# Prompt attention units dealt over the K pages and the V pages of a decoder layer, by one table of slots

## What is computed

```python
def layer_front(x, norm1_g, w_in, q_norm_g, k_norm_g):
    proj = rms_norm(x, norm1_g) @ w_in            # q, k, v, a, gate
    ...
    return q, k, v, a * jax.nn.sigmoid(gt)

# prompt: 8 heads, causal attention over the own and the past block of 256 keys (512 keys at most)
# sample: 2048 past keys in 16 pages of 128 keys per stream, best 3 blocks of 256 keys by q.mean(k),
#         plus the 4 new keys; pages are found by page_table
def conv_branch(u_ext, conv_w, conv_b, conv_norm_g):   # 31 taps, RMS norm over channels, swish
    ...
def layer_back(x, attn, conv, w_out, norm2_g, w_query, keys1, keys2, expert_u, expert_v):
    mix = jnp.concatenate([attn.reshape(x.shape[:-1] + (ATTN_WIDTH,)), conv], axis=-1)
    h = x + mix @ w_out
    return h + peer_ffn(rms_norm(h, norm2_g), w_query, keys1, keys2, expert_u, expert_v)
```

## Time and profile before

| what | value |
|---|---|
| time, median of 3 runs (lowest, highest) | 2172.93 us (2168.53, 2173.59) |
| the profiled execution's own time | 2174.22 us |
| its span, first to last instruction | 2172.6 us |
| mean granted TensorE clock | 0.964 |
| busy share of the span: TensorE matmul, weight load, VectorE, ScalarE, GpSimd | 93%, 88%, 63%, 34%, 35% |
| attention stage in the span | about 196 to 478 us |
| in it: K phase, to the last turn of a page | 196.0 to 372.5 us |
| in it: V phase, to the start of the last V chunk's product | 372.5 to 470.0 us |

### The profile page before, as it was taken

How to read it: one execution, slowest core, us unless ns; L and a number is a source line. 1 busy time by engine, 2 the same in 40 slices (tenths; PEclk the granted TensorE clock), 3 DMA queues, 4 the chain that set the end, 5 groups by cost and what they waited for, 6 DMA issues and landing times.

```text
span 2172.6 us, 39130 instructions
## 1 busy us (share of the span) xinstructions
PE 2025.2 (93%) x14822; PEld 1911.2 (88%) x14822; DVE 1371.3 (63%) x2452; ACT 729.7 (34%) x940; POOL 769.9 (35%) x493
## 2 busy tenths in 40 slices
PE   6878899768999999998899999999989999999999
PEld 6877667228999999998899999999989999999999
DVE  3869673301334457999888884200068988889885
ACT  3233565202222222322355554232222332333331
POOL 3222211323233333343321222333344555655550
PEclk9998999759999999999999999999999999999999
DMA  4252655971222333333244545533589999999993
GB/s 158 63 85 101 205 198 185 359 296 60 76 78 100 123 125 129 137 132 111 98 177 165 205 180 208 195 137 129 182 289 313 332 345 307 334 326 345 323 312 108
DMA packets 202168, 420.05 MB, mean 193 GB/s; under 512 B 28129, under 2 KB 137762, under 8 KB 189250
## 3 DMA queue, kind: packets, MB, share of 16 engines
q1 hardware_dynamic: 162866, 314.92, 42.1%
q0 software_dynamic: 32768, 100.75, 13.1%
q10 hardware_dynamic: 6416, 2.78, 1.0%
HBM read 350.46 MB, written 67.92 MB: 193 GB/s over the span
## 4 chain that ended last, share of the span: by engine, by line
PE 45%; issue 32%; DVE 9%; POOL 6%; DMA 3%; ACT 2%; DVEq 1%; SPq 1%; POOLq 1%; ACTq 0%
PE pair L1394 13%; PE pair L1396 12%; PE pair L1395 12%; POOL w_lo L552 6%; DVE conv L972 3%; PE pair L1539 2%; DVE pair L1355 1%; DVE w_lo L1338 1%; PE pair L1551 1%; DMA v_ring<-in_cache_v 1%; DMA picked_a<-acts,at_unit 1%; DMA page_ring<-in_cache_k 1%; PE pair L1504 1%; PE pair L1526 1%; DVEq L965 1%
## 5 line engine op out<-in xcount | busy, mean ns | idle before, releaser
L1394 PE MATMUL pair<-x_hi,w_hi 128*128 128x272 f32 x2560 | 757.4, 296 | 24.1 <-DVE x_lo L928 16.2
L1396 PE MATMUL pair<-x_hi,w_lo 128*128 128x272 f32 x2560 | 744.5, 291 | 0.0
L1395 PE MATMUL pair<-x_lo,w_hi 128*128 128x272 f32 x2560 | 741.0, 289 | 0.0
L552 POOL TENSOR_TENSOR w_lo<-w_raw,w_hi 128x2048 fp32r<-128x2048 f32 x64 | 301.3, 4707 | 621.7 <-ACT w_hi L798 621.7
L1394 PEld LDWEIGHTS pair<-x_hi,w_hi 128*128 128x128 f32 x2560 | 486.9, 190 | 27.7 <-issue 22.3
L1395 PEld LDWEIGHTS pair<-x_lo,w_hi 128*128 128x128 f32 x2560 | 487.1, 190 | 0.2
L1396 PEld LDWEIGHTS pair<-x_hi,w_lo 128*128 128x128 f32 x2560 | 485.7, 190 | 0.0
L1394 PE MATMUL pair<-a_hi,w_hi 128*128 128x416 f32 x1024 | 360.7, 352 | 13.1 <-DVE w_lo L1338 7.6
L1396 PE MATMUL pair<-a_hi,w_lo 128*128 128x416 f32 x1024 | 360.9, 352 | 0.0
L1395 PE MATMUL pair<-a_lo,w_hi 128*128 128x416 f32 x1024 | 358.2, 350 | 0.0
L816 ACT ACTIVATE act_out<-pair 128x544 f32<-128x544 f32 x128 | 81.3, 635 | 462.0 <-PE pair L1396 462.0
(11 more groups left out here) (199 smaller groups left out, 2644.4 us busy)
## 6 DMA issues: line engine op xcount, KB each, us to landing
w_raw<-in_u_t SPq DMA_DIRECT2D x64, 1024.0 KB, 5.8
acts<-act_out SPq DMA_DIRECT2D x64, 544.0 KB, 3.0
w_raw<-in_v_t SPq DMA_DIRECT2D x128, 256.0 KB
v_raw<-in_v_t SPq DMA_DIRECT2D x128, 256.0 KB, 5.9
gates<-g_out SPq DMA_DIRECT2D x13, 2048.0 KB, 8.0
g_in<-gates SPq DMA_DIRECT2D x16, 1664.0 KB, 13.3
act<-acts SPq DMA_DIRECT2D x64, 416.0 KB, 5.9
page_ring<-in_cache_k SPq DMA_DIRECT2D x64, 256.0 KB, 2.9
```

Source lines behind the costliest of these rows:

```text
L552: pool.tensor_tensor(w_lo[:, slot, :], w_raw[:, slot, :], w_hi[:, slot, :].bitcast(F32), ALU.subtract).then_inc(u_lo_done, 1)
L1394: te.matmul(out, s_hi, m_hi, start=start, stop=False)
L1395: te.matmul(out, s_hi, m_lo, start=False, stop=False)
L1396: return te.matmul(out, s_lo, m_hi, start=False, stop=stop)
```

## The change

A table `started` names the slot in which each prompt unit begins. 12 units begin in the K phase, at slots 2, 4, 7, 10, 12, 15, 18, 20, 23, 26, 28 and 31. The other 20 begin in the V phase, whose slots are counted from `FIRST_VALUES` (`at` = 0 to 31): at 0, 1, 2, 3, 5, 6, 7, 9, 10, 11, 13, 14, 15, 16, 18, 19, 20, 22, 23 and 24. All three engines now walk one loop over 65 slots, and one V chunk is attended in each slot of the V phase. The selection of batch 1, the convolution's norm and its swish stand at fixed slots of that loop. Since prompt units and V chunks now run together, the PSUM banks are dealt anew: probabilities are turned in banks 4 and 0, V products gather in bank 2, outputs are turned in bank 1, and the prompt keeps 3, 5, 6 and 7. `pages_pt` and `sqc` no longer lie over `q_t`, which the late units still read, but over the second halves of `w_hi` and `w_lo`. The number of matmuls, of activations and of VectorE operations on data stays the same; ScalarE's list has two more table loads.

```diff
@@ constants @@
+    S_TURN, O_TURN, O_OUT = (4, 0), 1, 2
...
+    FIRST_VALUES = CHUNKS + 1
+    LAST_SLOT = FIRST_VALUES + CHUNKS
...
+    KEY_UNITS, VALUE_SLOTS = 12, 26
+    started = {2 + CHUNKS * n // KEY_UNITS: n for n in range(KEY_UNITS)}
+    for n in range(UNITS - KEY_UNITS):
+        started[FIRST_VALUES + VALUE_SLOTS * n // (UNITS - KEY_UNITS)] = KEY_UNITS + n
@@ ScalarE @@
+            for t in range(LAST_SLOT):
+                if t < CHUNKS:
+                    keep_page(t, 0)
+                    keep_page(t, 1)
+                if t % 4 == 1 and 1 < t < CHUNKS:
+                    keep_scores(t // 4 - 1)
+                if t < CHUNKS:
+                    keep_page(t, 2)
+                    keep_page(t, 3)
+                if t in started:
+                    prompt_exp(started[t])
+                if t - 1 in started:
+                    prompt_keep(started[t - 1])
...
+                if t == CHUNKS:
+                    keep_scores(2 * PAGES // 4 - 1)
+                    keep_probabilities(0)
+                at = t - FIRST_VALUES
+                if at == 3:
+                    exp_rows(1)
+                if at in (4, 6, 8, 10):
+                    square_conv((at - 4) // 2)
+                if at == 13:
+                    root(pair[0], CH, sumc_done, CC, rootc_done)
+                if at == 15:
+                    sc.wait_ge(z_done, 1)
+                    for cc in range(CC):
+                        sc.activation(sig_c[:, cc, :], conv[:, cc, :], ACT.Sigmoid).then_inc(sigc_done, 1)
+                    keep_output(0)
+                    keep_probabilities(1)
@@ VectorE @@
+            for t in range(LAST_SLOT):
+                if started.get(t - 3, 0) % 2:
+                    prompt_mix(started[t - 3] // 2)
+                if t - 1 in started:
+                    prompt_norm(started[t - 1])
+                if t < CHUNKS:
+                    some_taps()
+                if t in started:
+                    prompt_max(started[t])
...
+                if at == 1:
+                    rows_mask(1)
+                if at == 2:
+                    rows_max(1)
+                if at == 5:
+                    rows_norm(1)
+                if at == 14:
+                    reciprocal_rms(rootc_done)
...
+                if 17 <= at < 17 + CC:
+                    finish_conv(at - 17)
@@ TensorE @@
             def turn_probabilities(b):
                 te.wait_ge(s_normed, b + 1)
+                if b:
+                    te.wait_ge(rootc_done, 1)
...
+            for t in range(LAST_SLOT):
+                if t < CHUNKS:
+                    turn_page(t, 0)
+                    turn_page(t, 1)
+                if t in started:
+                    prompt_scores(started[t])
+                if 1 <= t <= CHUNKS:
+                    score_chunk(t - 1)
+                if t - 1 in started:
+                    prompt_turn(started[t - 1])
+                if t < CHUNKS:
+                    turn_page(t, 2)
+                    turn_page(t, 3)
+                if t == CHUNKS:
+                    turn_probabilities(0)
+                at = t - FIRST_VALUES
+                if at >= 0:
+                    if at == PAGES:
+                        turn_probabilities(1)
+                    attend(at)
+                if t - 2 in started:
+                    prompt_values(started[t - 2])
+                if at in (5, 7, 9, 11):
+                    sum_block(pair[0], sqc, (at - 5) // 2, CC, sqc_done, sumc_done)
+                if at == PAGES + 2:
+                    turn_output(0)
```

More of the change, by code:

```diff
@@ L768, in _ @@
[L768 to L777 removed]
+                sc.activation(o_nat[:, :], bank(O_OUT), ACT.Copy).then_inc(o_kept, 1)
@@ L1120, in _, with finish_conv @@
                                 ALU.add).then_inc(own_kept, 1)
[L1121 to L1149 removed]
+            def finish_conv(cc):
                 v.wait_ge(sigc_done, cc + 1)
@@ L1153, in _ @@
                 parts(PAIRS + cc, conv[:, cc, :])
+            for t in range(LAST_SLOT):
[7 more added lines that the diff above has]
+                    prompt_max(started[t])
+                if t == PAGES + 2:
+                    rows_mask(0)
+                elif t == PAGES + 3:
+                    rows_max(0)
+                elif t == PAGES + 5:
+                    rows_norm(0)
+                at = t - FIRST_VALUES
+                if at == -1:
+                    assert next_tap == [TAPS, TAPS]
+                    v.drain()
+                    v.memset(stats[:, 56:57], 0.0).then_inc(conv_done, 1)
+                if at == 1:
[6 more added lines that the diff above has]
+                    reciprocal_rms(rootc_done)
+                    for cc in range(CC):
+                        last = v.scalar_tensor_tensor(conv[:, cc, :], conv[:, cc, :], conv_g[:, cc:cc + 1], rstd[:, :],
+                                                      ALU.mult, ALU.mult)
+                    last.then_inc(z_done, 1)
+                if 17 <= at < 17 + CC:
+                    finish_conv(at - 17)
             mix_output(0)
```

129 lines of the change are left out of this document (34 added, 95 removed).

## The result

The changed kernel takes **2184.84 us** (median of 5 runs, 2182.11 to 2188.78), the kernel before 2172.17 us (5 runs, 2168.53 to 2173.59). The ratio is 1.0061, 95% interval 1.0047 to 1.0075: slower by 12.7 us, where 6 us faster was forecast, and above the forecast's range. The profiled execution of the changed kernel has an own time of 2184.84 us and a span of 2183.2, the one of before 2174.22 and 2172.6, so the two profiles differ by 10.6 us.

The account below looks back on a forecast made before the run. K phase bound by the ring of two in early slots and TensorE in late ones, V phase near its DMA limit; 2174.2 - 23.1 (K phase) + 16.8 (V phase) = 2167.9 us own time, 2167 as median, 8 us to either side.

Parts of the forecast that it names:

- K phase: 29 slots at 4.6 us from 209.7; last page's turn ends at 349.4 instead of 372.5, 23.1 us gained.
- Head of the V phase: From the last turned K page to the first V product: 6.9 us.
- TensorE's work: V phase: products of chunks 0 to 25 23.4 us, units 41.4, convolution's sums and other turns 8.4.
- Waits: V phase: TensorE stops at units' turns for VectorE's norms, and V products stand behind; 21.2 us together.
- Clock: V phase: wait gaps bring 1.2 GHz windows; at a mean clock of 0.97 for 73 us of work, 2.5 us.
- rival 3: V phase: TensorE at half speed after long waits, mean clock 0.8, about 8 us longer; time about 2173, chance 0.16.
- Tail: End of the V phase: after product 25 ends, the last chunk lands about 10.5 us later.
- Behind the last product: From the last V product to the output projection: nothing changes.
- the first: V phase: units hide under the V transfers, so it stays as long as it is; 2150 us, chance 0.22.
- The second: K phase: the ring keeps its pace of 5.16 us a slot; kernel 8.4 us slower, 2181, chance 0.17.
- My own bound: Prediction wrong if the K pace is above 5.0, or the V phase below 105 or above 122 us.

Follow-up runs that it names:

- fill: The changed kernel with idle turns of the identity on TensorE in the longest waits of the V phase; 2177.2 us, ratio 1.0016 to the kernel before.
- wlate: The changed kernel with the output projection's two weight loads held back until V chunk 29's product is done; 2187.9 us, ratio 1.0059 to the kernel before.
- kfill: The changed kernel with five idle turns on TensorE ahead of each wait for a K page; 2182.9 us, ratio 1.0050 to the kernel before.
- attfirst: The changed kernel with each V product ahead of the previous unit's turn in the V phase; 2174.7 us, ratio 1.0008 to the kernel before.
- klate: The changed kernel with all four quarters of a K page turned ahead of the chunk's scores and the unit's turn; 2167.7 us, ratio 0.9965 to before.
- k32klate: The changed kernel with all 32 units in the K phase and klate's order there; 2165.6 us, ratio 0.9966 to the kernel before.

## Why the prediction was wrong

I forecast an own time of 2167.9 for the profiled execution and got 2184.84. The step that failed is the term for TensorE's clock in the V phase. Step by step, in the order of the prediction:

- **K phase, 349.4 forecast, 352.7 measured: 3.3 late.** Chunk 2 began at 206.2, not 209.7. The pace was 4.82 a slot in place of 4.6 (with 1.5 each for the selection and the clock, 4.70). And the last slot took 6.6 us (346.1 to 352.7), not 3.3: its page landed late and the turns ran at 1.2 GHz. The other six profiles of this order end 0.5 to 9.6 us later still, so the miss of this term may be larger than this profile shows. The turn-round was taken from two values, 5.3 and 6.5, as if they alternated.
- **Head of the V phase, 6.9 forecast, 7.0 measured** (352.7 to 359.7). Right.
- **TensorE's work, 23.4 + 41.4 + 8.4 = 73.2 forecast, 76.9 measured.** From the first product to the end of product 25 (359.7 to 463.6, 103.9 us) TensorE is busy for 86.4 us; less half of the 19.1 us at 1.2 GHz, 9.5, this is 76.9. Most of the difference is the product: I wrote 0.9 for two in 1.92; in a slot it occupies 1.0, from its start to the start of what follows, which is 2.6 us over 26 of them.
- **Waits, 21.2 forecast, 17.5 measured** (103.9 - 86.4). The mechanism, the places and the longest (5.6 forecast, 5.2 measured behind the reciprocal) were right. What was too high was the wait behind ScalarE ahead of V chunk 16: 3.8 forecast, 0.4 measured, for TensorE had its own work there, most of it at half speed, from 418.1 to 429.6, and ScalarE waited 3.84 us for it at 427.3. The waits of batch 1's exponentials were 1.25 and not 2.5, that of unit 14 nothing and not 1.3. At full clock (fill) the waits and the idle turns in them are 20.1, close to the forecast. The Trainium skill, "ScalarE: Activation LUTs", section "What ACT_TABLE_LOAD costs", puts about 2.66 us on each change of table. Here a table load is 1.28 and begins 0.02 us or less after the instruction ahead of it, so the trace does not show the drain, and this is not where the miss lies:

```profile
407.65 0.19 ACT L708 ACTIVATION_READ_ACCUMULATOR p_nat<-pair,stats 128x1 f32 x1
407.86 1.28 ACT L609 ACT_TABLE_LOAD   x1
409.15 0.71 ACT L609 ACTIVATE rstd<-pair,eps 128x544 f32<-128x544 f32 x1
409.88 1.28 ACT L708 ACT_TABLE_LOAD   x1
```

- **Clock, 2.5 forecast, 9.5 measured.** This is the step that failed. "At a mean clock of 0.97" was a guess that no row bore; the profile of before had 0.68 in this phase. I had put it down as rival 3 with 8 us and a chance of 0.16, as if it were apart from the waits. It is not: fill shows that the same kernel without the low clock needs 97.3 us (369.4 to 466.7) where the forecast less its clock term has 94.4. Net of the waits that the slow work covers, the clock cost 103.9 - 97.3 = 6.6 us. The two prices that I gave it did not follow my own rule either: 73 us of work at a mean clock of 0.97 become 2.3 longer, and at rival 3's 0.8 they become 18 longer and not 8. At the 0.89 that was measured the rule gives 9.0.
- **Tail, 10.5 forecast, 14.8 measured** (463.6 to 478.4). In these 14.8 us TensorE is busy for 7.9: two units' values are still to come, the chunks' loads go out in a burst, and the output projection's two loads of 1.0 MB share the engines. wlate shows 2.2 us of the 4.3 (12.6 from product 25's end in its profile), nearer 1.6 against the average of the other profiles. I had counted the DMA engines as free for V pages. No run shows what the rest is.
- **Behind the last product, nothing forecast, 2.2 measured**: 8.9 in place of 8.5 us to the output projection. The rest is in stages that the change does not touch and that differ as much between the profiles of all versions (1513.1 to 1518.4 us from the first instruction that writes act_out to the end, 1516.1 in before and 1518.4 in the change).

3.3 + (3.7 - 3.7 + 7.0) + 4.3 + 0.1 + 2.2 = 16.9, the whole difference between 2167.9 and 2184.84. The clock is the largest part of it, 7.0, and not all: with that term right the forecast would have been 2174.9, still 9.9 too low, through the tail (4.3), the K phase (3.3) and what lies behind the last product (2.2). That TensorE's work was 3.7 too low and the waits 3.7 too high, so that the two cancel, is luck. One more slip: the two K slots of before add up to 10.4 us, not 10.3, which changes nothing in the 5.2 a slot.

Of the rivals, the first fell: the V phase was not hidden under its transfers, whose DMA share dropped to 0.80. The second came nearest in time (2181), with the wrong mechanism: the pace was 4.82 and not 5.16, at which I had said that the two phases cancel, and raising the clock of the K phase to 0.98 (kfill) brought no gain clear of the spread. The third had the mechanism that held, slow work behind long waits. It forecast 2173, because its 8 us stood alone. The Trainium skill's section "HAM oscillation — how this bites in real kernels", in "TensorE: Matmul & The Clock Gate", was weighed for the K phase, where taking the low clock away gave nothing measurable. It tells of waits for DMA; up to product 25 of the V phase the trace shows the same behind waits for VectorE, after the two longest alone (3.41 and 5.22 us). The work behind the waits of 1.39 us at 433.25 and 461.97 ran at full clock. My own bound, a V phase above 122 us, is what was crossed.

## What to carry to other kernels

A wait on TensorE that is forecast at several microseconds has two prices, its length and the half-speed work behind it; write the second as a term worked out from the clock of the rows nearest to it, never as a small remainder. Part of it can come back, where the slow work covers later waits (9.5 us of it cost 6.6 here). When work is moved under a transfer, put the consumer of the transfer ahead of the moved work in each engine's list (attfirst: 10 us), and look for the slot where several long pieces of other engines meet. Before sharing work between two phases, ask what releases the ring of the lighter one: here an order of three steps within a slot (klate) gave 17 us, where the move lost 13, and 7 us without the move (k32klate).

## What the runs showed of the hardware that was not expected

- **Work that nobody reads can make the kernel faster.** 94 idle turns in five waits of the V phase gave 7.6 us (fill). In the K phase the same means raised the clock from 0.92 to 0.98 and gave nothing that can be told from the spread (kfill).
- **Slow landings go along with instruction packets.** In the K phase of the changed kernel a chunk's pages take 4.73 to 6.69 us from issue to landing. Counted over chunks 4 to 31, from a chunk's first issue to its last landing, the median is 5.02 us for the 9 chunks that had no packet of the "instruction" kind under way on the DMA queues meanwhile and 5.66 for the 19 that had one; for before it is 4.93 (12) and 6.12 (16), for wlate 4.84 (8) and 6.03 (20). The queues of the changed kernel from 338 to 347 us, where the last chunk's pages landed at 346.0, 6.7 us after their issue:

```profile
q0 software_dynamic: 257, 0.81, 22.9%
q1 hardware_dynamic: 302, 0.55, 19.8%
q8 instruction: 1, 0.02, 0.7%
```

A longer landing also has more chances to meet a packet, and no run varied the packets alone. That they delay the pages is argued, not shown, and it stays open, as does the spread of the K phase between profiles of one kernel.
